# Splitting the streamed weight tiles on ScalarE and VectorE instead of GpSimd

## What is computed

```python
x = x + g1 * ((sigmoid(ga) * (attention(h) @ w_attn_out) + sigmoid(gv) * conv(h)) @ w_mix_out)   # windowed attention
x = x + g2 * peer(rmsnorm(x))     # 8 heads x 16 experts for each token: rows of two tables of 16384 x 1024
y = rmsnorm(x)
for layer in range(2):
    y = layer_norm(ALPHA * y + mixer(y))            # layer 0: mLSTM, layer 1: four windowed means and a product
    y = layer_norm(ALPHA * y + cross_attention(y))  # 4 heads, 256 memory rows
    y = layer_norm(ALPHA * y + mlp(y))              # 1024 -> 4096, relu squared -> 1024
```

## Time and profile before

| | |
|---|---|
| three runs, us | 3495.84, 3497.38 (median), 3499.48 |
| profiled execution, us | 3496.58, span 3494.8, mean granted clock 0.928 |
| PE busy | 2945.1 us, 84% |
| DVE busy | 2257.4 us, 65% |
| POOL busy | 1856.1 us, 53% |
| ACT busy | 926.1 us, 26% |
| DMA | 719.21 MB, 206 GB/s over the span |
| of POOL: upper parts (L398) | 548.1 us, 277 of 1979 ns |
| of POOL: lower parts (L401) | 718.2 us, 277 of 2593 ns |
| of POOL: gather issues (L428) | 564.1 us, 512 of 1102 ns |

### The profile page before, as it was taken

One profiled execution on the slowest core, in us unless ns is written; L12 is line 12 of the kernel. 1 busy time (PEld: TensorE's weight loads), 2 busy tenths in 40 slices (PEclk: granted clock), 3 DMA queues, 4 the chain that ended last, 5 costly groups with the idle time before them and its releaser, 6 DMA issues. The chain is left out here.

```text
span 3494.8 us, 33128 instructions
## 1 busy us (share of the span) xinstructions
PE 2945.1 (84%) x10628; PEld 1938.5 (55%) x10628; DVE 2257.4 (65%) x3761; ACT 926.1 (26%) x2350; POOL 1856.1 (53%) x1099
## 2 busy tenths in 40 slices
PE   6889898877778877888877779979899975889998
PEld 5667676632333323444433267657678864667886
DVE  7793464376666667776766583675855577586556
ACT  2115402233433333333333322221200012220001
POOL 2544375464444444666554264254577763557874
PEclk9899899999999999999999989989999987999998
DMA  5531122699999999999999811011122220112221
GB/s 216 185 113 55 43 79 73 241 421 419 413 418 412 412 422 409 391 389 399 390 422 418 341 66 55 31 60 61 60 90 96 91 72 12 61 60 93 94 96 55
DMA packets 126107, 719.21 MB, mean 206 GB/s; under 512 B 13200, under 2 KB 16400, under 8 KB 60176
## 3 DMA queue, kind: packets, MB, share of 16 engines
q0 software_dynamic: 73728, 536.90, 37.4%
q1 hardware_dynamic: 46560, 161.18, 13.4%
q10 hardware_dynamic: 5680, 19.40, 1.5%
HBM read 715.33 MB, written 2.10 MB: 205 GB/s over the span
## 5 line engine op out<-in xcount | busy, mean ns | idle before, releaser
L712 PE MATMUL psum<-slots,acc 128*128 128x512 f32 x2048 | 1016.2, 643 | 267.9 <-ACT acc L1167 267.4
L398 POOL TENSOR_TENSOR whi<-w,zeros 128x1024 fp32r<-128x1024 f32 x277 | 548.1, 1979 | 883.1 <-PE psum L469 566.4
L428 POOL DMA_INDIRECT slots<-in_experts,consts x512 | 564.1, 1102 | 675.0 <-PE psum L712 603.5
L1719 DVE SCALAR_TENSOR_TENSOR arena<-slots,work 128x1024 f32<-128x1024 f32 x512 | 663.2, 1295 | 400.1 <-DMA slots<-in_experts,consts 383.1
L712 PEld LDWEIGHTS psum<-slots,acc 128*128 128x128 f32 x2048 | 393.7, 202 | 868.5 <-ACT acc L1167 462.3
L401 POOL TENSOR_TENSOR wlo<-w,whi 128x1024 fp32r<-128x1024 f32 x277 | 718.2, 2593 | 21.7
L467 PE MATMUL psum<-xhi,whi 128*128 128x512 f32 x1104 | 451.5, 409 | 8.7 <-POOL wlo L401 5.6
L468 PE MATMUL psum<-xlo,whi 128*128 128x512 f32 x1104 | 441.8, 400 | 0.0
L469 PE MATMUL psum<-xhi,wlo 128*128 128x512 f32 x1104 | 440.5, 399 | 0.0
L467 PE MATMUL psum<-yhi,whi 128*128 128x512 f32 (+1 forms) x736 | 300.1, 408 | 49.9 <-POOL ylo L453 20.7
L468 PE MATMUL psum<-ylo,whi 128*128 128x512 f32 (+1 forms) x736 | 296.2, 402 | 0.0
(11 more groups left out here) (266 smaller groups left out, 3671.3 us busy)
## 6 DMA issues: line engine op xcount, KB each, us to landing
w<-in_stream SPq DMA_DIRECT2D x277, 512.0 KB
arena<-in_wmod SPq DMA_DIRECT2D x4, 2048.0 KB, 17.8
arena<-in_wmod ACTq DMA_DIRECT2D x8, 1024.0 KB, 6.1
acc<-in_wmod ACTq DMA_DIRECT2D x8, 1024.0 KB, 8.3
slots<-in_experts,consts POOLq DMA_INDIRECT x512
xres<-in_xT SPq DMA_DIRECT2D x1, 2048.0 KB, 15.3
outT<-xres SPq DMA_DIRECT2D x8, 256.0 KB, 2.0
consts<-in_consts SPq DMA_DIRECT2D x1, 1056.0 KB, 5.2
```

What stands on the lines that cost most here:

```text
L398: pool.tensor_tensor(hi, w32[:, s, :], zeros[:, :].broadcast_to((P, 1024)), ALU.add)\
L428: pool.indirect_dma_start(out=slots[p % SLOTS], out_offset=None, in_=a["experts"], in_offset=bass.IndirectOffsetOnAxis(ap=indices[:, p:p + ...
L712: mm = pe.matmul(bank(4 + half), diag[:, p % 2, :], v[:, half * T:(half + 1) * T], start=(c == 0), stop=(c == PICKS - 1))
L1719: dve.scalar_tensor_tensor(dot_out, slots[p % SLOTS][:, 0:D], 1.0, tokens[:, p // PICKS, :], ALU.mult, ALU.mult, accum_out=inner[:, c:c + ...
```

## The change

POOL no longer splits weight tiles. ACT writes the upper part with a Copy activation (`upper`), DVE the lower part with a subtraction (`lower`), which waits for the upper part; the waits on the load, on `tile_done` and the signals `w_upper` and `w_split` stay as they were. POOL keeps the gathers and its three feature tiles. Since ACT and DVE have one list each, 277 calls of `upper` and of `lower` are written into their lists. `upper(n + RING)` stands behind the ACT instruction that takes product n, in the norm stages behind a square (`also`); `lower` follows on DVE at a place of the same stage.

```diff
@@ gpsimd
-            def split_tile(s, n, nth, reused):
-                pool.wait_ge(w_loaded[s], nth * 16)
-                if reused:
-                    pool.wait_ge(tile_done, n + 1 - RING)
...
-                pool.tensor_tensor(hi, w32[:, s, :], zeros[:, :].broadcast_to((P, 1024)), ALU.add)\
-                    .then_inc(sem("w_upper"), 1)
-                pool.wait_ge(sem("w_upper"), n + 1)
-                pool.tensor_tensor(lo, w32[:, s, :], hi.bitcast(F32), ALU.subtract).then_inc(w_split, 1)
...
             for p in range(NPICKS):
                 gather(p)
-                if 16 <= p < 48 and p % 8 == 0:
-                    m = (p - 16) // 8
-                    split_tile((n + m) % RING, n + m, (n + m) // RING + 1, True)
-                m = (p - MEM_AT - 10) // MEM_EVERY
-                if p >= MEM_AT + 10 and (p - MEM_AT - 10) % MEM_EVERY == 0 and m < 2 * KB:
-                    split_tile((n + RING + m) % RING, n + RING + m, (n + RING + m) // RING + 1, True)
-            split_tiles(n + RING + 2 * KB, mixed)
@@ scalar
+            def upper(n, turn=0):
+                if n >= NTILES:
+                    return
+                s = n % RING
+                act.wait_ge(w_loaded[s], turn * 64 + 16 * (n // RING + 1))
+                if n >= RING:
+                    act.wait_ge(tile_done, turn * 16 + (n + 1 - RING))
+                act.activation(whi[:, s, :, :].rearrange("p k n -> p (k n)"), w32[:, s, :], ACT.Copy)\
+                    .then_inc(sem("w_upper"), 1)
...
             root(1)
+            for m in range(RING):
+                upper(m)
...
             for i in range(5):
                 raw(i, o + 1 + i)
+                upper(n + i + RING)
...
                 attn_slot(i)
+                upper(SECTIONS[f"conv{i}"][0] + RING)
...
                     copy_product(mem_raw[:, m % 2, :], o + m, CT)
+                    upper(n + m + RING)
...
                 copy_product(lraw[:, m % 2, 3:3 + T], o + m)
+                upper(n + m + RING)
                 if m:
                     silu(m - 1)
...
                     copy_product(xq[:, m, :], oo)
+                    upper(n + m + RING)
...
+                def hidden_group(half, turn):
+                    for k in range(4):
+                        relu(o + 4 + 12 * half + k, False, 4 + 4 * half + k, turn)
+                        upper(n + 4 + 8 * half + k + RING, turn)
+                    for k in range(4):
+                        upper(n + 8 + 8 * half + k + RING, turn)
@@ vector
+            def lower(n, turn=0):
+                if n >= NTILES:
+                    return
+                s = n % RING
+                dve.wait_ge(sem("w_upper"), turn * 16 + (n + 1))
+                dve.tensor_tensor(wlo[:, s, :, :].rearrange("p k n -> p (k n)"), w32[:, s, :],
+                                  whi[:, s, :, :].rearrange("p k n -> p (k n)").bitcast(F32), ALU.subtract)\
+                    .then_inc(w_split, 1)
...
                 if g == 1:
                     statistics(1, EPS)
+                    for m in range(RING):
+                        lower(m)
...
                 dve.wait_ge(sem("rotated"), i + 1)
+                lower(n + i + RING)
                 if i:
                     mod_pair_dots(i - 1)
+            lower(n + 5 + RING)
...
                 attn_slot(i)
+                lower(SECTIONS[f"conv{i}"][0] + RING)
...
             pick_experts(0)
+            for m in range(9, 16):
+                lower(n + m)
             pick_gates(0)
...
+                m, at = (p - MEM_AT) // MEM_EVERY, (p - MEM_AT) % MEM_EVERY
+                if 0 <= m < 2 * KB and at == 4:
+                    lower(first_tile("memk") + m + RING)
...
+                for j in range(2):
+                    lower(n + 2 * h + j + RING)
             head_stats(3)
...
                     if k:
                         add_square(ni, k - 1)
+                        lower(n + k - 1 + RING)
...
                 statistics(ni, LN_EPS, mean=True)
+                lower(n)
...
                         hidden(o + 4 + 12 * half + j, 4 * (1 - half) + j, 4 + 4 * half + j, turn=g)
+                        lower(n + 4 + 8 * half + j + RING, g)
                     for k in range(KB):
...
                         free(dve.tensor_tensor(acc[:, k, :], acc[:, k, :], bank(oo % RING), ALU.add), oo)
+                        if k % 2:
+                            lower(n + 8 + 8 * half + k // 2 + RING, g)
```

More of the change, by code:

```diff
@@ L1110, in _ @@
                 attn_slot(12 + i)
+                upper(n + i + RING)
             for i in range(28, 34):
                 attn_slot(i)
-            squares(2, lambda k: xres[:, k, :], ready=lambda k: wait_read(act, SECTIONS["mix"][1] + k))
+            for m in range(KB):
+                upper(first_tile("branch") + m + RING)
+            squares(2, lambda k: xres[:, k, :], ready=lambda k: wait_read(act, SECTIONS["mix"][1] + k),
+                    also=lambda k: upper(first_tile("mix") + k + RING))
             root(2)
@@ L1281, in read_of, with upper_after @@
                 return lambda k: wait_read(act, o + k)
-            post_norm(4, 0, read_of(SECTIONS["lout"][1]))
+            def upper_after(n, per=1):
+                return lambda k: upper(n + k // per + RING) if k % per == per - 1 else None
+            n, o = SECTIONS["lout"]
+            post_norm(4, 0, read_of(o), also=upper_after(n))
             ni = 4
@@ L1351, in _ @@
                     relu(o + k, layer == 0 and k < 2, k)
-                with act.Fori(0, 3) as g:
-                    for half in range(2):
-                        for k in range(4):
-                            relu(o + 4 + 12 * half + k, False, 4 + 4 * half + k, g)
-                for k in range(4):
-                    relu(o + 76 + k, False, 28 + k)
-                post_norm(ni + 2, 3 * layer + 2, read_of(o + 88), last=(layer == 1))
+                    upper(n + k + RING)
+                def hidden_group(half, turn):
[4 more added lines that the diff above has]
+                        upper(n + 8 + 8 * half + k + RING, turn)
+                with act.Fori(0, 3) as g:
+                    hidden_group(0, g)
+                    hidden_group(1, g)
+                hidden_group(0, 3)
+                post_norm(ni + 2, 3 * layer + 2, read_of(o + 88), last=(layer == 1), also=upper_after(n + 60, 2))
         @block.vector
@@ L1606, in _ @@
                 attn_slot(i)
+                if i < 28:
+                    lower(first_tile("gates") + i - 12 + RING)
             n, o = SECTIONS["branch"]
@@ L1732, in _ @@
             dve.tensor_copy(identr, ident).then_inc(sem("ident_ready"), 1)
+            n = first_tile("pq") + RING
+            for m in range(5):
+                lower(n + m)
             top_keys(0)
+            lower(n + 5)
+            lower(n + 6)
             top_pairs(0)
+            lower(n + 7)
+            lower(n + 8)
             pick_experts(0)
+            for m in range(9, 16):
+                lower(n + m)
             pick_gates(0)
@@ L1797, in _ @@
             dve.tensor_scalar(mrow, mrow, -1.0, None, ALU.mult).then_inc(sem("floor_arg"), 1)
+            for m in range(8, 17):
+                lower(first_tile("lstm") + m + RING)
             dve.wait_ge(sem("decay_turned"), 1)
@@ L2019, in _ @@
                         add_square(ni + 2, k - 1)
+                    if k in (1, 3, 5):
+                        lower(n + 60 + k // 2 + RING)
                 add_square(ni + 2, KB - 1)
                 step.settle()
[L2022 removed]
+                post_norm(ni + 2, n + 63 + RING, last=(layer == 1))
 def shape_constants():
```

73 lines of the change are left out of this document (41 added, 32 removed).

## The result

The changed kernel takes 3340.8 us (3339.5 to 3341.3, four runs) against 3496.6 us (3494.2 to 3499.5, four runs) for the kernel before, taken on the same chip: a ratio of 0.9554, 95% interval 0.9537 to 0.9570. That is 156 us less; 3370 had been forecast, and 3341 lies inside the range of 3332 to 3410. The profiled execution took 3341.3 us, its span is 3339.2 us.

A forecast was written before the change was run, and what follows sets the result against it. No engine bounds the whole; where PE waits, it waits for VectorE, slowed by GpSimd beside it. Stage gains sum to 126.5 us, taken from 3496.6 us for 3370 us; 8-in-10 range 3332 to 3410.

The forecast's parts named there:

- First projections: Tiles 0 to 5: mod products and rotations lose their excess, lowers add 6; the last rotation ends about 8 us earlier.
- Convolution: Convolution stage, 12 slots: DVE falls to 7.6 us a slot, PE becomes the bound at 106 us; gain 26 us.
- Query projection and first gathers: Gathers outside the memory tiles already run at 415 GB/s with full DMA share: gain 0.
- Heads: Four mLSTM heads: one slow cast a head speeds up, two lowers cost 2 x 1.22 us; gain 1 us.
- Memory stage: 128 gathers, 361.0 us: transfer rate rises from 393 towards 415 GB/s; half taken, gain 10 us, ends 0 and 19.
- Tails and MLPs: Norm tails with the pooling norm 28.5 us, cross attention softmax waits 6, MLP starts 18.
- Gates: Gates and branch: PE is full there, so gain 0.
- rival B: More comes back: memory stage 9 us more, PE clock 15, taps' stage 10; 3336 us, chance 0.15.
- Rivals A: Less comes back: convolution loses 14 us, memory stage 10, gathers held up 11; 3405 us, chance 0.14.
- C: Memory stage: DVE stands waiting for ACT's upper, gather slots run dry, 10 + 80 us lost; 3460 us, chance 0.06.
- E: No measurable effect: GpSimd's work is not what slows VectorE; chance 0.02.
- Rival D: Steady MLP: parts come too late for the ring's 16.8 us, PE stops each tile; 3562 us at 1.5 us, chance 0.04.

The follow-up runs named there:

- the first experiment: Changed kernel plus two unused 128x1024 GpSimd additions per weight tile outside pick loop, mLSTM projections and heads; 3527.8 us.
- the mixed version: Changed kernel with lower parts of tiles 4 to 53 and 111 to 126 on GpSimd; 3336.2 us, later 3334.2 against 3339.9 us.
- the experiment with the 16 tiles: Changed kernel with both parts of the 16 tiles split between picks 298 and 418 back on GpSimd; 3355.8 us.

## Why the prediction was right, and where it was off

The mechanism is the one forecast, and it is now shown by the first experiment instead of argued: VectorE was slow because GpSimd stood beside it. 126.5 us were forecast, 155.6 came (spans 3494.8 and 3339.2), 29 us more; the terms were sized too small in the heads, the memory stage and the norms and MLPs. Term by term, from the start of one stage's products to the next's:

```
term                                     forecast   measured
start                                       6          7.4
first projections                           8          5.2
convolution                                26         28.8
gates, branch                               0         -1.4
merge, norm 2                               3          3.4
query projection and gathers to memk        0          3.8
memory tiles, gathers up to the mLSTM      10         18.0
mLSTM projections                          20         19.1
heads                                       1          8.8
norm tails, cross attention, MLPs          52.5       62.6
```

- **Prices of the new operations**: right, 1.055 for a forecast of 1.06 us, and 1.22 for 1.22.
- **First projections**: the rotation's wait gave 7.0 us for a forecast of 8, but the next wait, for ScalarE, grew by 2.3.
- **Convolution**: "So PE becomes the bound: 12 x 8.8 = 106" was right, 103.7 came, at 8.6 a slot; VectorE was busy for 91.5 us of it, for which 92 had been put down.
- **Query projection and first gathers**: put at 0, 3.8 came. The step that failed is "Gathers outside the memory tiles: 415 GB/s at full DMA share, 0": it looked at the rate of the later gathers alone. In the kernel before, GpSimd splits four tiles between picks 16 and 41, from 690.6 to 757.5, with the gathers standing behind them. With their lower parts on GpSimd at the same places, 3.6 of the 3.8 us are gone again.
- **Heads**, the largest miss for its size: 1 forecast, 8.8 came. The step was that the two lowers a head "cost 2 x 1.22 on the same chain" and take back what the cast gives. The chain was not what PE waited for. PE waited 4.5 us for the small products that mask the diagonal (0.29 us alone, up to 1.82 beside GpSimd), in waits of at most 1.7 us that have no line in the earlier trace rows, and lost about as much in granted clock. The lowers stand where PE has other work. The clock's part is not certain from one profile: in the mixed version's second profile, where GpSimd does nothing in the heads and PE does not stop, the stage has 5.4 us at the lower clock and takes 2.5 us more.
- **Memory stage**: "I take half, 10". The ends were 0 and 19, and 16.9 came by the stage's own picks: the splits had most of the blame, 11.7 us in the profile of the experiment with the 16 tiles and 15 us by the medians. The half was a guess between two bounds, and the forecast says so. The bound of 11 us the other way, that lowers hold up the issue, did not show in the time: 15 issues beside a lower part took 3 us more in all, and the queue did not run empty.
- **Tails and MLPs**: the MLPs' products gave 11.2 and 11.1 us for 9 each, the tail behind the first 10.0 for 8.5, since it fell to 5.9 us rather than to 6.8 to 8, and the two cross attentions with their tails 7.9 and 6.8 for 5 each. The 7 us of the pooling norm came as 6.1, by luck: its own wait for the sums gave 2.4 (12.4 to 10.0), and 3.7 came in the pooling's products, which had been put at 0.
- **Gates**: "PE full, 0" holds for the products (136.6), but the attention's tail behind them is 1.9 us longer, at a granted clock of 0.62 where it was 0.74 (first before, then after):

```profile
401.30:438.10 36.80, 25.42 (x138) 20.68 (x139) 16.48 (x49) 10.64 (x23) 4.25 (x2) 0.74 0.05 15
...
359.40:398.10 38.70, 28.98 (x137) 23.71 (x138) 17.67 (x51) 11.47 (x24) 0.00 (x0) 0.62 0.09 28
```

  PE's idle time there fell from 11.4 to 9.7 us; what grew is its busy time, for the same matmuls. With the lower parts on GpSimd gates and tail were 3.2 us shorter than in the changed kernel, at a higher clock; why the clock differs so is not shown.
- **Clock**: TensorE spent 507.7 us at the lower of its two levels before and 382.3 us after, the mean granted clock rose from 0.928 to 0.943. The forecast has the clock only as part of two terms; rival B had more of it, with the memory stage's other half. Of that half 7 of 9 us came, the clock rose, and the taps' stage did not end sooner than forecast; the time ended 5 us from rival B's 3336. What the clock gave beyond the forecast was not measured apart.

Rivals A, C and E are out: PE is busy throughout the convolution stage, the gathers' queue is never empty in the memory stage, where VectorE waits 3.9 us in all for upper parts, and the change is measurable. ScalarE loads a function table 89 times in either kernel, so the uppers brought no such load. Rival D did not come in the changed kernel: PE waits twice for a lower part, 3.7 us together.

Open are why the granted clock differs in the gates' tail, and how much of the mixed version's missing gain is more than scatter.

## What to carry to other kernels

Before giving GpSimd elementwise work "for free", look at the mean time of one shape on VectorE in a stretch with and without GpSimd: an operation whose time jumps by up to the length of GpSimd's instruction is likely waiting for it. If the work must stay there, use short instructions, let it meet operations of VectorE that read PSUM, and keep long stretches of it out of the queue that issues gathers (a pair of 5.0 us cost 12 us over 16 places here, a single operation of 2.5 us nothing). And price a move of work by what waits at each place: the same half of the work on GpSimd cost 5 us or 88, depending on which half.

## What the runs showed of the hardware

- A cast of 128x512 takes 0.43 us alone and ends 0.28 us behind the GpSimd tensor_tensor during which it started, a 128x512 tensor_tensor of two SBUF inputs 0.55 us behind, one of 128x1024 1.08 us behind (medians of 55, 151 and 122 cases of the first experiment, which lie within 0.03 us of them): each waits for the whole instruction. GpSimd waits in turn: 1.9 to 2.0 us for 159 additions beside nothing, and 2.8 for 82 of the 141 that start during a lower part of VectorE.
- A tensor_tensor of VectorE with one input in PSUM is never held up (0 of 99 beside additions, 0 of 211 beside tensor_scalars), and one with two SBUF inputs not by a memset (0 of 157), while the cast is (74 of 75).
- GpSimd's tensor_scalar of 128x1008 takes 2.7 us and holds up two-input operations only when they start in its first 0.8 us (75 of 85, later 0 of 250).
- Halving GpSimd's instruction halves the wait of a cast that meets it: it takes 1.15 us beside 128x512 additions, 2.00 beside 128x1024. What is lost in all falls less, since more operations meet one of the shorter instructions.
